# A two-block transformer kernel: reordering TensorE, VectorE and ScalarE work in its first even mixer

## The reference

```python
def ab_mixer(xn, w_in, ...):
    proj = xn @ w_in                       # 1024 -> x 512, g 512, q and k 512 each, v 512, o 512, 4 + 4 gates
    xa, ga, qk, v, o, i_pre, f_pre = jnp.split(proj, cuts, axis=-1)
    ya = jax.nn.gelu(ga) * rglru(causal_dwconv(xa, rg_conv_w, rg_conv_b), ...)
    yb = mlstm_block(qk, v, o, i_pre, f_pre, ...)
    return jnp.concatenate([ya, yb], axis=-1) @ w_out

# rglru:  r, ig = sigmoid(blocks of x @ w_r), sigmoid(blocks of x @ w_i)
#         a = exp(-8 r softplus(-lam)); u = sqrt(1 - a*a) * ig * x; h = scan(a, u)
# mlstm:  q, k = silu(conv(qk)); chunks of 128 tokens, 4 heads of 128
#         m, d from cumulated log gates; p = exp(d - m) * (q k^T)
#         num = carried state * q + p v; den likewise; h = num / max(|den|, exp(-m))
#         h = h * rsqrt(mean(h*h) + eps) * norm_g; yb = sigmoid(o) * h
```

## Time and profile before

| what | us |
|---|---|
| median of 3 runs | 2216.4 (2214.45 to 2216.63) |
| the profiled execution | 2214.61 |
| its span | 2212.8 |
| TensorE busy | 2145.3 (97%) |
| VectorE busy | 1558.9 (70%) |
| ScalarE busy | 1295.9 (59%) |
| POOL busy | 91.6 (4%) |

### The profile page before, as it was taken

The page is one execution under the profiler, slowest core; times in us unless marked ns, Lnnn a source line. Parts: engine busy times, 40 slices in busy tenths (PEclk is TensorE's granted clock), DMA queues, the critical chain, the costliest instruction groups (busy, mean ns, idle before and its releaser), DMA issues.

```text
span 2212.8 us, 33168 instructions
## 1 busy us (share of the span) xinstructions
PE 2145.3 (97%) x12373; PEld 1842.7 (83%) x12373; DVE 1558.9 (70%) x2766; ACT 1295.9 (59%) x2160; POOL 91.6 (4%) x52
## 2 busy tenths in 40 slices
PE   8999989999999989999999998999999999989998
PEld 7888978888888976888788896878887888978886
DVE  6777777677767476767777766577666766867765
ACT  6665766556555266655665566446555655656554
POOL 0001000000002220000000001100000000000001
PEclk9999999999999999999999989999999999999999
DMA  6453344554553442455455331135544553434552
GB/s 265 181 198 149 136 162 178 193 198 169 183 192 146 165 143 77 173 199 199 153 200 186 148 129 39 58 133 208 192 158 171 202 197 142 169 121 174 196 194 81
DMA packets 64954, 362.97 MB, mean 164 GB/s; under 512 B 7512, under 2 KB 8280, under 8 KB 32792
## 3 DMA queue, kind: packets, MB, share of 16 engines
q1 hardware_dynamic: 64368, 360.31, 44.3%
q10 hardware_dynamic: 296, 0.27, 0.0%
q0 software_dynamic: 128, 0.26, 0.0%
HBM read 359.77 MB, written 1.05 MB: 163 GB/s over the span
## 4 chain that ended last, share of the span: by engine, by line
PE 81%; DVE 11%; ACT 5%; issue 1%; DMA 0%; POOL 0%; DVEq 0%; ACTq 0%; SPq 0%; POOLq 0%
PE ps L202 79%; DVE WL L120 5%; ACT work L192 2%; PE ps L207 2%; DVE work L120 2%; ACT WH L192 2%; ACT XBt L192 1%; DVE XBt L131 1%; DVE small L131 1%; DVE small L120 1%; DVE work L131 1%; DVE work L157 0%; DVE work L125 0%; DVE small L127 0%; DMA ring<-wts 0%
## 5 line engine op out<-in xcount | busy, mean ns | idle before, releaser
L202 PE MATMUL ps<-XBt,WH 128*128 128x512 f32 (+1 forms) x4208 | 1216.4, 355 | 16.2 <-DVE WL L120 7.0
L120 DVE TENSOR_TENSOR WL<-ring,WH 128x1024 fp32r<-128x1024 f32 x636 | 786.7, 1237 | 375.1 <-ACT WH L192 331.9
L192 ACT ACTIVATE WH<-ring 128x1024 fp32r<-128x1024 f32 x664 | 703.4, 1059 | 362.8 <-PE ps L202 302.3
L202 PE MATMUL ps<-XBt,WL 128*128 128x256 f32 x3384 | 897.5, 281 | 0.0
L202 PEld LDWEIGHTS ps<-XBt,WH 128*128 128x128 f32 x4208 | 732.2, 191 | 124.8 <-DVE XBt L131 13.1
L202 PEld LDWEIGHTS ps<-XBt,WL 128*128 128x128 f32 x3384 | 643.3, 190 | 26.2
L202 PE MATMUL ps<-WH,HHt 128*128 128x512 f32 x712 | 279.5, 393 | 1.3 <-DVE WL L120 1.1
L202 PE MATMUL ps<-WL,HHt 128*128 128x512 f32 x712 | 277.2, 389 | 0.0
L202 PE MATMUL ps<-WH,HLt 128*128 128x512 f32 x712 | 274.6, 389 | 0.0
L192 ACT ACTIVATE work<-ps 128x256 f32<-128x256 f32 (+5 forms) x450 | 182.2, 412 | 68.4 <-PE ps L202 37.3
L192 ACT ACTIVATE work<-work 128x256 f32<-128x256 f32 (+6 forms) x222 | 98.8, 445 | 180.3 <-DVE work L120 175.8
(11 more groups left out here) (133 smaller groups left out, 1202.9 us busy)
## 6 DMA issues: line engine op xcount, KB each, us to landing
ring<-wts SPq DMA_DIRECT2D x248, 1024.0 KB, 5.8
ring<-wts SPq DMA_DIRECT2D x179, 512.0 KB, 3.8
ring<-wts SPq DMA_DIRECT2D x1, 1152.0 KB, 5.0
ct<-cons SPq DMA_DIRECT2D x1, 1086.5 KB, 5.8
Xt<-x SPq DMA_DIRECT2D x4, 256.0 KB, 5.7
out<-Xt SPq DMA_DIRECT2D x4, 256.0 KB, 2.0
work<-wts SPq DMA_DIRECT2D x1, 512.0 KB, 5.0
ring<-wts SPq DMA_DIRECT2D x2, 256.0 KB, 2.7
```

Source lines behind the costliest of these rows:

```text
L120: self.done(self.e and self.e.tensor_tensor(out, a, b, op), inc)
L192: self.done(self.e and self.e.activation(out, a, f, **kw), inc)
L202: inst = self.e and self.e.matmul(out, l, r, start=start, stop=stop)
```

## The change

Seven edits, all in the lists of the first even mixer:

1. The row of the norm: TensorE does row_pe between the two halves u of ab_x.1 and no longer ahead of it; VectorE fills BD, XPX and XPQ and makes the low part of ab_if before it copies the row.
2. `tms_pe` calls `between` after each half. col_pe and the first spread (ab.m0) stand behind ab_v.0, the second (ab.m1) between the halves of ab_v.1. The banks of the values are therefore taken before those of col_pe and the spreads.
3. ScalarE does two gates, then the high parts of ab_v.1, then the other two gates, where it did four gates and then the high parts.
4. The high parts of ab_g.1 move from ScalarE to VectorE (`hi_dve`), each half followed by its low part.
5. On ScalarE, YH comes behind the copies of TOT and the first high part of ab_w0.0; the second high part of ab_w0.0 and the split of the second pair come before the squares and sigmoid of ab_o.0.
6. On VectorE, ya1 comes before the wait for yh0; yl0, the second low part of ab_w0.0 and yl1 come before the chain of roots.
7. On VectorE, the product HT comes before the low part of the first half of ab_w1.0.

```diff
--- before.py
+++ after.py
@@ -387,6 +387,12 @@
                     E.tt(wl, w, wh.bitcast(F32), SUB, inc=f"{name}:lo{part}")
 
 
+        def hi_dve(V, name, part):
+
+            wh, _, w = cut(name, part)
+            V.wait_ge(loaded(name, part), gone(ahead(name, -2), part))
+            V.cp(wh, w, inc=f"{name}:hi{part}")
+
         def cm_pe(P, piece, t, head=None, between=None):
 
 
@@ -425,10 +431,10 @@
                             key = (piece if i else f"{piece}:i0") if j == nk - 1 else None
                             P.mm3(ps[f"{last}/{i}"][:, 0:n], XH[:, kt, hs(i)], XL[:, kt, hs(i)], wh[:, j * n:j * n + n],
                                   wl[:, j * n:j * n + n], kt == 0, kt == 7, inc=key)
+                        if between:
+                            between(P, c, i)
                     if head and c == 0 and js[0] == 0:
                         head.pe(P, 1)
-                if between and piece != last:
-                    between()
             for i in range(2):
                 ps.give(f"{last}/{i}", f"{last}.e{i}")
 
@@ -1110,8 +1116,16 @@
                         P.tr(ps["ab.col"][:, o:o + 4], R(3 + qn, c * 128, c * 128 + 128), IDN[0:4, 0:4],
                              inc="ab.col" if qn and c else None)
                 ps.give("ab.col", "ab.col.e")
-                for c in range(2):
-                    cast_pe(P, f"ab.m{c}", R(2, c * 128, c * 128 + 128), f"ab.m{c}.e", "ab.r5")
+
+            def stretch_pe(P, c):
+                cast_pe(P, f"ab.m{c}", R(2, c * 128, c * 128 + 128), f"ab.m{c}.e", "ab.r5")
+
+            def beside_values_pe(P, c, i):
+                if (c, i) == (0, 1):
+                    col_pe(P)
+                    stretch_pe(P, 0)
+                if (c, i) == (1, 0):
+                    stretch_pe(P, 1)
 
             def gates_pe(P):
                 P.wait_ge("ab.bd00", "ab.bd01", "ab.bd10", "ab.bd11")
@@ -1192,8 +1206,7 @@
 
             def pe(P):
                 cm_pe(P, "ab_x.0", t, norm)
-                row_pe(P, t)
-                cm_pe(P, "ab_x.1", t)
+                cm_pe(P, "ab_x.1", t, between=lambda P: row_pe(P, t))
                 if_pe(P)
                 cm_pe(P, "ab_q.0", t)
                 if_turn_pe(P)
@@ -1202,8 +1215,7 @@
                 gates_pe(P)
                 rows_pe(P)
                 cm_pe(P, "ab_k.1", t)
-                col_pe(P)
-                tms_pe(P, ("ab_v.0", "ab_v.1"), 4, 512, t)
+                tms_pe(P, ("ab_v.0", "ab_v.1"), 4, 512, t, between=beside_values_pe)
                 kt_pe(P)
                 for c in range(2):
                     kq_pe(P, c)
@@ -1244,8 +1256,8 @@
                 A.wait_ge(f"{piece}.cv")
                 A.act(d, d, ACT.Silu, inc=f"{piece}.si")
 
-            def gates_act(A):
-                for c in range(4):
+            def gates_act(A, cs):
+                for c in cs:
                     A.wait_ge(f"ab.rg{c}")
                     A.act(T1[:, c, :], ps[f"ab.rg{c}"][:, 0:256], ACT.Tanh, scale=0.5, bias=hbr[:, c:c + 1], back=1 + min(c, 1))
                     A.act(GX[:, c, :], ps[f"ab.rg{c}"][:, 256:512], ACT.Tanh, scale=0.5, bias=hbi[:, c:c + 1], inc=f"ab.rg{c}.e", back=2)
@@ -1293,8 +1305,9 @@
                 A.act(R(3), R(3), ACT.Exp)
                 A.act(R(4, 128, 256), R(2, 128, 256), ACT.Exp, scale=-1.0, bias=m0, back=2)
                 A.act(R(4, 0, 128), R(1, 0, 128), ACT.Exp, bias=nm0, inc="ab.r7", back=3)
-                gates_act(A)
+                gates_act(A, (0, 1))
                 hi(A, ahead("ab_k.1"))
+                gates_act(A, (2, 3))
                 taps_act(A, "ab_k.1")
                 silu_of(A, "ab_q.0")
                 silu_of(A, "ab_q.1")
@@ -1308,7 +1321,6 @@
                 for i in range(2):
                     A.wait_ge("ab_v.1" if i else "ab_v.1:i0")
                     A.act(V1[:, i, :, 0:128], v3(ps[f"ab_v.1/{i}"], 4), ACT.Copy, scale=n_r[:, i:i + 1], inc=f"ab_v.1.e{i}")
-                hi(A, ahead("ab_v.1"))
                 A.wait_ge("ab.kt", "ab.col.e")
                 for h in range(4):
                     A.act(KW[:, hs(h)], ps["ab.kt"][:, hs(h)], ACT.Copy, scale=col(1, 0, h), inc="ab.kw" if h == 3 else None,
@@ -1323,22 +1335,22 @@
                 hi(A, ahead("ab_g.1"))
                 for q in range(2):
                     gated_act(A, f"ab_g.{q}", GA, ACT.Gelu_apprx_tanh)
-                A.wait_ge("ab.ya0")
-                A.act(YH, Y8[:, 0:2, :], ACT.Copy, inc=f"{t}.yh0")
                 for c in range(2):
                     for pr in range(2):
                         A.wait_ge(f"ab.tv{c}{pr}")
                         A.act(TOT[:, 4 * c + 2 * pr:4 * c + 2 * pr + 2, :], v3(ps[f"ab.tv{c}{pr}"][:, 0:258], 2), ACT.Copy,
                               inc=f"ab.tv{c}{pr}.e")
                 hi(A, ahead("ab_o.0"), (0,))
+                A.wait_ge("ab.ya0")
+                A.act(YH, Y8[:, 0:2, :], ACT.Copy, inc=f"{t}.yh0")
+                hi(A, ahead("ab_o.0"), (1,))
+                in_act(A, t, 1, Y8, "ab.ya1", "ab_o.1")
                 for j in range(8):
                     if j == 4:
-                        hi(A, ahead("ab_o.0"), (1,))
                         A.wait_ge("ab.tc0.e", "ab.tc1.e")
                     A.act(HT[:, hs(j)], TOT[:, j, 0:128], ACT.Square, accum_out=sq[:, j:j + 1], inc="ab.hs" if j == 7 else None,
                           back=4 if j else 1)
                 gated_act(A, "ab_o.0", OO, ACT.Sigmoid)
-                in_act(A, t, 1, Y8, "ab.ya1", "ab_o.1")
                 hi(A, ahead("ab_o.1"))
                 gated_act(A, "ab_o.1", OO, ACT.Sigmoid)
                 for i in range(2):
@@ -1384,13 +1396,13 @@
                         lo(V, "ab_x.0")
                     if q == 3:
                         lo(V, "ab_x.1", (0,))
-                row_dve(V, t)
                 V.set(BD, 0.0)
                 V.set(XPX[:, :, 0:4], 0.0)
                 V.set(XPQ[:, :, 0:4], 0.0, inc="ab.z")
                 lo(V, "ab_x.1")
                 V.wait_ge("ab_if:hi")
                 V.tt(wil, raw("ab_if"), wif.bitcast(F32), SUB, inc="ab_if:lo")
+                row_dve(V, t)
                 conv_rows_dve(V, "ab_x.0")
                 lo(V, ahead("ab_x.0"))
                 taps_dve(V, "ab_x.0")
@@ -1439,7 +1451,9 @@
                 for c in range(2):
                     V.wait_ge(f"ab.ex{c}")
                     V.tt(v3(EX[c], 4), v3(EX[c], 4), over(triT, 4, 128), MUL, back=1 + c)
-                lo(V, ahead("ab_v.1"))
+                for part in range(2):
+                    hi_dve(V, ahead("ab_v.1"), part)
+                    lo(V, ahead("ab_v.1"), (part,))
                 for c in range(2):
                     V.wait_ge(f"ab.kq{c}")
                     V.stt(EX[c], ps[f"ab.kq{c}"], SQ, EX[c], MUL, MUL, inc=f"ab.pe{c}", back=1 + c)
@@ -1456,10 +1470,8 @@
                 lo(V, ahead("ab_g.1"))
                 V.wait_ge("ab_g.0.th")
                 V.tt(YA[:, 0:2, :], GA[:, 0:2, :], XC[:, 0:2, :], MUL, inc="ab.ya0")
-                V.wait_ge(f"{t}.yh0")
-                V.tt(YL, Y8[:, 0:2, :], YH.bitcast(F32), SUB, inc=f"{t}.yl0")
                 V.wait_ge("ab_g.1.th")
-                V.tt(YA[:, 2:4, :], GA[:, 2:4, :], XC[:, 2:4, :], MUL, inc="ab.ya1")
+                V.tt(YA[:, 2:4, :], GA[:, 2:4, :], XC[:, 2:4, :], MUL, inc="ab.ya1", back=2)
                 for pr in range(2):
                     V.wait_ge(f"ab.tc{pr}", f"ab.tv1{pr}.e")
                     for u in range(2):
@@ -1467,22 +1479,24 @@
                         V.stt(TOT[:, 4 + h, :], ps[f"ab.tc{pr}"][:, u * 129:u * 129 + 129], col(1, 1, h), TOT[:, 4 + h, :], MUL, ADD,
                               inc=f"ab.tc{pr}.e" if u else None, back=1 + u)
                 lo(V, ahead("ab_o.0"), (0,))
+                V.wait_ge(f"{t}.yh0")
+                V.tt(YL, Y8[:, 0:2, :], YH.bitcast(F32), SUB, inc=f"{t}.yl0")
+                lo(V, ahead("ab_o.0"), (1,))
+                in_dve(V, t, 1, Y8)
                 V.stt(dd, TOT[:, :, 128], -1.0, TOT[:, :, 128], MUL, MAX)
                 V.tt(dd, dd, COL[:, 0:8], MAX)
                 V.rec(dd, dd)
                 rows_dve(V, "ab_o.0", OO[:, 0:2, :])
-                lo(V, ahead("ab_o.0"), (1,))
                 V.wait_ge("ab.hs")
                 V.tt(sq, sq, dd, MUL)
                 V.tt(sq, sq, dd, MUL)
                 V.ts(x4, sq, 1.0 / 128, EPS, MUL, ADD)
                 V.rsqrt(y4, x4, t4)
                 V.tt(y4, y4, dd, MUL)
-                in_dve(V, t, 1, Y8)
-                lo(V, ahead("ab_o.1"), (0,))
                 for c in range(2):
                     V.tt(v3(HT, 8)[:, 4 * c:4 * c + 4, :], TOT[:, 4 * c:4 * c + 4, 0:128], each(y4[:, 4 * c:4 * c + 4], 4, 128), MUL,
                          inc=f"ab.hn{c}", back=1 + c)
+                lo(V, ahead("ab_o.1"), (0,))
                 rows_dve(V, "ab_o.1", OO[:, 2:4, :])
                 lo(V, ahead("ab_o.1"), (1,))
                 for i in range(2):
```

## The result

| | kernel before | changed kernel |
|---|---|---|
| median, 8 runs each | 2213.3 (2211.0 to 2216.6) | 2207.9 (2205.7 to 2210.2) |
| profiled execution | 2214.61 | 2207.15 |
| its span | 2212.8 | 2205.3 |

The ratio is 0.9969, with a 95% interval of 0.9960 to 0.9978: 6.9 us, between 4.9 and 8.9. The two medians of eight differ by less, 5.4 us. I had forecast 7.5 us and 2208.9. The kernel before came out at 2213.3 with five more runs, where the first three had 2216.4. The profiled executions differ by 7.46.

What follows compares the result with a forecast made beforehand. TensorE, busy 2145.3 of 2212.8 us, was taken as the bound, so only its waits and low clock could be won. Terms reached 4.0 us by ab_o.1 and 7.5 in all: 2216.4 to 2208.9, range 2205.8 to 2212.6.

Steps and rivals of the forecast that it cites:

- The sum: All gains inside the first even mixer, up to the next norm's transposes: 7.5 us.
- The forecast case: Whole mixer: the 7.5 us gain arrives, median 2208.9 us, own range 2207 to 2210.5; chance 0.60.
- the new waits: TensorE on the way back: 1.5, 0.2 and 0.8 us within 3.5 us; rival that the clock falls there, 2210.5, chance 0.20.
- the row: Norm's row at ab_x.1: 1.80 us of wait and 1.7 of low clock go, together 3.5 us.
- thin products: col_pe and spreads among the values: a 0.38 us wait goes, two operand changes cost 0.2, net gain 0.2.
- high parts on VectorE: ab_g.1's copies: 0.84 us each, ready near 267.9 before TensorE wants them at 269.6, so hidden; ScalarE loses 2.15 us.
- way back: From ab_o.1 to the next norm's transposes: second quarter of w0 11.6 us early, partly given back; sum from 4.0 to 7.5.
- ab_o.1's wait: TensorE's 0.28 us wait for ab_o.1's low part goes, because the scans end 6 us earlier; sum 4.0.
- VectorE's idleness before AL*AL: VectorE's 2.45 us of idleness behind ScalarE's decay acts mostly goes.
- its four waits: TensorE on the way back: 1.5 us before HT's transposes, 0.8 for w1.0's low part, 1.0 and 0.7 in back_pe.
- the wait of 3.56: TensorE before w0's second quarter, at 301.31: this wait goes, and the quarter takes 2.72 us instead of 5.26.
- VectorE keeps the gain: Rival, from ab_o.1's end: VectorE has the same work in either order, so only 4.0 us remain, 2212.4; chance 0.10.

Runs made afterwards that it cites:

- the squares: Changed kernel with ScalarE's squares ahead of yh1, ab_w1.0's high parts ahead of ab_o.0's sigmoid, first three root operations ahead of yl1: D 115.05 us, ratio 0.9959.
- the split scaling: Changed kernel with the squares ahead of yh1, plus the second half of HT's scaling on ScalarE instead of VectorE: D 114.42 us, ratio 0.9968.

## Why the prediction was right, and where its steps were not

**The sum** was 7.5; D fell by 7.06, the profiled executions differ by 7.46, the ratio says 6.9. The forecast case came in; in its two profiles the clock did not fall in the new waits. That the time, 2207.9, lies only 1.0 below the forecast 2208.9 is in part luck: the base of 2216.4, from three runs, was 3.1 above that of eight, and the gain was put 2.1 above the difference of the medians. From 2213.3 the same sum gives 2205.8.

**Terms against prices.** The sum is nearly right, and its division among the parts is not:

| part | booked | undone, by D | undone, by the ratio |
|---|---|---|---|
| the row (edit 1) | 3.5 | 2.1 | 2.9 |
| thin products (edits 2, 3) | 0.2 | 2.8 | 4.4 |
| high parts on VectorE (edit 4) | 0 (hidden) | 2.6 | 3.3 |
| way back (edits 5 to 7) | 3.5 (7.5 - 4.0) | 0.85 | 2.7 |

The 0.3 that is missing from 7.5 is ab_o.1's wait, which I booked for VectorE's lead as a whole.

**The norm's row.** "1.80 for the wait and 1.7 for the clock" fits the profiled executions: ab_if starts 3.57 us earlier (3.74 less 0.17 of start). But the second term was a matter of that execution: in both other profiles with this wait (1.81 and 1.80) the clock held. As an average it had to be counted by a chance, not in full.

**The thin products.** "Net gain 0.2" is the step that failed in attribution. The sum stood, since I had put kt_pe 3.7 early and it came 3.6 early; but it comes so early only with edits 2 and 3 beside edit 1 (0.97 with edit 1 alone). I priced the edit against the wait of before (0.38), while the row's edit would have made it 1.4 and, in both profiles that have these waits, a fallen clock. Priced in the new schedule it is 2.8.

**The high parts on VectorE.** "Hidden" was right for TensorE's wait for ab_g.1 (none); its worth lay in ScalarE's 2.15 us, 1.8 at the transposes and 2.6 with the clock, which I had put down to no part at all. I had seen that VectorE's idleness before AL*AL would go, and had not made a term of it.

**The way back.** The forecasts of its four waits were each within 0.25. The booking was wrong: from 4.0 at the end of ab_o.1 to 7.5 I put 3.5 us down to this part, most of it the wait of 3.56 and its clock. Much of that was VectorE's lead from the front, which the old lists turn into almost the same end (0.85 by D, in an execution in which the clock fell at their wait of 3.67). The ratio leaves room for up to the whole 3.5 in the average execution. That the new lists win the rest by giving the clock no wait of 3.6 us to fall behind is plausible and not shown.

**The parts overlap.** Undone one at a time they cost 2.1 + 2.8 + 2.6 + 0.85 = 8.4 of D against the 7.06 of all together. By the ratios it is 13 against 6.9, too rough to be added up but in the same direction.

**The rival "VectorE keeps the gain"** was nearer to the truth than its 0.10 says: VectorE is what the way back hangs on, as the squares and the split scaling show. It fails on its number, because VectorE itself had come 5.7 us earlier.

What stays open: how much of each ratio is the clock. The single profiles say where it fell in one execution each; the share of executions in which it falls at each place was not measured. Nor were edits 2 and 3, or 5, 6 and 7, undone one by one; the prices are those of the groups.

## What to carry to other kernels

Price each part of a reordering in the schedule that the other parts leave, not in the one before: an edit that only moved a wait of 0.4 in the old schedule was worth 2.8 us in the new one. Before giving work to the engine that looks idle, see which engine heads the chain at that place, and whether the idle engine shares something with the one you relieve. When one profile says little (0.85) and the whole times say more (2.7), look where the profiled execution lies among the others before trusting it. A long wait of TensorE may be worth removing even where the time reappears as shorter waits: here the clock fell behind every wait of 1.83 us or more on the way back, and behind two of the six of 1.36 to 1.62.

## What the runs showed of the hardware that was not expected

- POOL and VectorE excluded each other in float32 operations with two inputs in SBUF: 0.17 us became 2.40, and 2.4 became 3.41. The Trainium skill ("GPSIMD Engine Reference", section "8. Key points") names contention of POOL with VectorE's instructions that have two inputs in SBUF. These runs agree, and show the size: in six overlaps the operation that began later took longer by what the other still had to run, less 0.12 to 0.15 us (2.23 of 2.38 and 1.02 of 1.16 in the two large ones).
- The same wait of 1.8 us before the same product was followed by a granted clock of 0.66 over five microseconds in one kernel's profile and of 1.00 in two others' (edit 1 undone, and edits 5 to 7 alone). On the way back, waits of 1.83 to 3.67 us were followed by a low clock in all five profiles that have one; waits of 1.36 to 1.62, with 0.67 a little later, in two of six.
- VectorE's copy of 128x1024 from float32 to float32r in SBUF takes 0.69 us, where the subtraction of the same size takes 1.23 and ScalarE's copy 1.06.
